# A two-block hybrid layer on one core: gated-convolution units and their projection move in between the steps of the state-space scan, dt is computed with the tokens streaming, and x is kept in DRAM meanwhile

## The reference, cut to what matters

```python
def hybrid_mixer(h, w_in, ssd_conv_w, ssd_conv_b, dt_bias, a_log, d_skip, ssd_norm_w,
                 w_ssd_proj, sconv_w, w_sconv_proj, w_o):
    u = h @ w_in
    z, xbc, dt_raw, s_b, s_c, s_x, g_a, g_b = jnp.split(u, IN_SPLITS, axis=-1)
    xbc = jax.nn.silu(causal_depthwise_conv(xbc, ssd_conv_w) + ssd_conv_b)
    xs, bm, cm = jnp.split(xbc, (SSD_INNER, SSD_INNER + SSD_GROUPS * SSD_STATE), axis=-1)
    ...
    dt = jax.nn.softplus(dt_raw.astype(jnp.float32) + dt_bias.astype(jnp.float32))
    ...
    y = ssd_chunked_scan(xs32, dt, a, bm32, cm32)
    y = y + d_skip.astype(jnp.float32).reshape(SSD_GROUPS, SSD_HPG)[..., None] * xs32
    y = y.reshape(bsz, seqlen, SSD_INNER) * jax.nn.silu(z.astype(jnp.float32))
    ...
    yg = yg * lax.rsqrt(jnp.mean(yg * yg, axis=-1, keepdims=True) + EPS)
    y = (yg.reshape(bsz, seqlen, SSD_INNER) * ssd_norm_w.astype(jnp.float32)).astype(h.dtype)
    branch_a = y @ w_ssd_proj
    v = causal_depthwise_conv(s_c * s_x, sconv_w)
    branch_b = (s_b * v) @ w_sconv_proj
    merged = jax.nn.sigmoid(g_a) * branch_a + jax.nn.sigmoid(g_b) * branch_b
    return merged @ w_o
```

## Time and profile before

| | us |
|---|---|
| median of 3 runs | 1913.37 |
| lowest and highest | 1910.51, 1920.85 |
| span of the profiled execution (first to last instruction) | 1916.4 |
| mean granted TensorE clock, share of full speed | 0.96 |
| busy in the span: TensorE, VectorE, ScalarE, GpSimd | 1783.9, 713.0, 709.4, 718.3 |

### The profile page before, as it was taken

The page is one execution under the profiler, slowest core; times in us unless marked ns, Lnnn a source line. Parts: engine busy times, 40 slices in busy tenths (PEclk is TensorE's granted clock), DMA queues, the critical chain, the costliest instruction groups (busy, mean ns, idle before and its releaser), DMA issues.

```text
span 1916.4 us, 22407 instructions
## 1 busy us (share of the span) xinstructions
PE 1783.9 (93%) x7678; PEld 1393.4 (73%) x7678; DVE 713.0 (37%) x1021; ACT 709.4 (37%) x894; POOL 718.3 (37%) x302
## 2 busy tenths in 40 slices
PE   3999797999999979999997998989899999999997
PEld 1777574888888848888875776767687788888885
DVE  5556415111110043320046988878411422222101
ACT  3455325434433342233233333433522344434322
POOL 1322033444446634444222222222444344444563
PEclk7999798999999989999898999999999999999998
DMA  8343221322223313222112111111222222222331
GB/s 324 143 154 132 99 66 44 99 89 97 88 73 97 93 66 99 88 96 94 62 55 66 59 52 56 55 44 55 77 89 99 88 88 88 90 96 82 84 97 66
DMA packets 50503, 171.93 MB, mean 90 GB/s; under 512 B 5610, under 2 KB 5866, under 8 KB 50322
## 3 DMA queue, kind: packets, MB, share of 16 engines
q1 hardware_dynamic: 50450, 171.27, 27.1%
HBM read 169.15 MB, written 2.10 MB: 89 GB/s over the span
## 4 chain that ended last, share of the span: by engine, by line
PE 80%; DVE 12%; ACT 3%; issue 3%; DMA 1%; DVEq 1%; SPq 0%; POOL 0%; ACTq 0%
PE PR L401 24%; PE PR L403 24%; PE PR L402 24%; DVE seg L1415 2%; DVE cx L1286 1%; DVE macc L1097 1%; PE AX L488 1%; DMA cond<-wcond 1%; PE AX L410 1%; PE AX L580 1%; PE AX L459 1%; PE AX L632 1%; DVE cx L1282 1%; DVE yb L1336 1%; DVE seg L1396 1%
## 5 line engine op out<-in xcount | busy, mean ns | idle before, releaser
L340 POOL TENSOR_TENSOR wlo<-raw,whi 128x1024 fp32r<-128x1024 f32 x288 | 701.8, 2438 | 1132.6 <-ACT whi L745 1132.6
L745 ACT ACTIVATE whi<-raw 128x1024 fp32r<-128x1024 f32 x288 | 302.9, 1052 | 196.3 <-PE PR L403 181.8
L401 PE MATMUL PR<-h3h,whi 128*128 128x512 f32 x640 | 263.9, 412 | 11.0 <-ACT xr L952 6.6
L402 PE MATMUL PR<-h3l,whi 128*128 128x512 f32 x640 | 256.7, 401 | 0.0
L403 PE MATMUL PR<-h3h,wlo 128*128 128x512 f32 x640 | 256.5, 401 | 0.0
L401 PEld LDWEIGHTS PR<-h3h,whi 128*128 128x128 f32 x640 | 122.6, 192 | 52.5 <-issue 20.4
L401 PE MATMUL PR<-hf1h,whi 128*128 128x512 f32 x352 | 141.1, 401 | 4.6 <-DVE hf1l L1083 3.9
L403 PEld LDWEIGHTS PR<-h3h,wlo 128*128 128x128 f32 x640 | 122.6, 192 | 29.9
L402 PEld LDWEIGHTS PR<-h3l,whi 128*128 128x128 f32 x640 | 122.8, 192 | 27.8 <-issue 0.7
L402 PE MATMUL PR<-hf1l,whi 128*128 128x512 f32 x352 | 140.6, 399 | 0.0
L403 PE MATMUL PR<-hf1h,wlo 128*128 128x512 f32 x352 | 140.4, 399 | 0.0
(11 more groups left out here) (257 smaller groups left out, 2872.0 us busy)
## 6 DMA issues: line engine op xcount, KB each, us to landing
raw<-w SPq DMA_DIRECT2D x224, 512.0 KB, 3.3
cond<-wcond SPq DMA_DIRECT2D x48, 512.0 KB, 4.3
raw<-w SPq DMA_DIRECT2D x32, 384.0 KB, 3.1
raw<-w SPq DMA_DIRECT2D x32, 320.0 KB, 2.9
x<-xin SPq DMA_DIRECT2D x1, 2048.0 KB, 7.6
out<-mixf SPq DMA_DIRECT2D x8, 256.0 KB, 2.0
con<-cons SPq DMA_DIRECT2D x1, 288.0 KB
att<-atts SPq DMA_DIRECT2D x1, 256.0 KB
```

Source lines behind the costliest of these rows:

```text
L340: pool.tensor_tensor(wlo[:, j, :], raw[:, j, :], whi[:, j, :], ALU.subtract).then_inc(lo_ready, 1)
L401: pe.matmul(bank, whi[:, j, w], oh[:, k0 + k, :], start=first and k == 0, stop=False)
L402: pe.matmul(bank, whi[:, j, w], ol[:, k0 + k, :], start=False, stop=False)
L745: act.activation(whi[:, j, :], raw[:, j, :], ACT.Copy).then_inc(hi_ready, 1)
```

## The change

- The order of the 104 mixer units is a list. First the dt sums, then B and C of group 0 and the convolution tiles 0 and 1 (8 units); then the 16 steps, each with one item of `BESIDE` between its parts: a convolution tile (3 units) in six steps, B and C of the next group in three (steps 3, 7, 11), a gate and projection unit pair in seven; then the last pair and the merge, with two g_a units in front of the first y unit.
- A step is: xs unit, `ssd_second` of the step before, first filling unit, (group start), second filling unit if there are three, z unit, `ssd_first`, last filling unit, `ssd_states`. Nothing stands at a unit's middle any more. The loops of the mixer are written out.
- dt: the weight (128x128 with zeros beside its 32 columns) is stationary and 512 tokens stream, 24 matmuls; ScalarE copies 32 rows out, four transposes turn them.
- B and C are read where they lie (bcm), without copies bt, ct, dag; bcm also takes the merge's tiles and lies where x was. So x is written to DRAM on SyncE's queue before the unit loads from 105 on and read back to x_re after the last g_a unit.
- The sum of a group's squares and `rms` move behind the next group's first step's states and behind gz.
- The output projection's first unit waits tile by tile for ml.

The diff, cut:

```diff
+BESIDE = {0: ("sc", 2), 1: ("sc", 3), 2: ("sc", 4), 3: ("bc", 1), 4: ("sc", 5), 5: ("sc", 6), 6: ("sc", 7), 7: ("bc", 2),
+          8: ("pj", 0), 9: ("pj", 1), 10: ("pj", 2), 11: ("bc", 3), 12: ("pj", 3), 13: ("pj", 4), 14: ("pj", 5), 15: ("pj", 6)}
+PARTS_OF = {"sc": ("c", "x", "b"), "bc": ("B", "C"), "pj": ("gb", "pj")}
...
 @block.sync
-            stream(U_SC, U_DN2, 32)
+            for n, (kind, m) in enumerate(MIXER):
+                first, step = W8_OF[kind]
+                load_unit(U_SC + n, (U_SC + n) % RING, w8_at(first + step * m))
+                if n == 4:
+
+                    for ready, count in (shared(res_ready, res_pool, 1, KT - 1), shared(res_ready, res_pool, 1, BY_POOL[-1])):
+                        sp.wait_ge(ready, count)
+                    sp.dma_start(x_keep[:, :, :], x[:, :, :]).then_inc(s_keep, 16)
+            for u in range(U_WO, U_WO + RING):
+                load_unit(u, u % RING, w8_at(u - 32))
+
+            sp.wait_ge(unit_used, AT["ga", KT - 1] + 1)
+            sp.wait_ge(s_keep, 16)
+            sp.dma_start(x_re[:, :, :], x_keep[:, :, :]).then_inc(s_back, 16)
+            stream(U_WO + RING, U_DN2, 32)
...
 @block.tensor
+            def dt_sums():
+
+                pe.wait_ge(dt_v, 1)
                 for k in range(KT):
+                    pe.wait_ge(*lo_part(2, k))
                     for n, (hx, wx) in enumerate(((h3h, wdth), (h3l, wdth), (h3h, wdtl))):
-                        mm = pe.matmul(AX[:, 0, 32 * c:32 * c + 32], hx[:, k, c * P:(c + 1) * P], wx[:, k, :],
-                                       start=k == 0 and n == 0, stop=k == KT - 1 and n == 2)
+                        mm = pe.matmul(AX[:, 1, :], wx[:, k, :], hx[:, k, :], start=k == 0 and n == 0,
+                                       stop=k == KT - 1 and n == 2)
+                mm.then_inc(dt_done, 1)
...
+            dt_sums()
+            mixed(("B", 0))
+            dt_turn()
+            mixed(("C", 0))
+            for name in beside("sc", 0):
+                fill(name)
+            dt_running()
+            for name in beside("sc", 1):
+                fill(name)
             pe.wait_ge(sel_ready, 1)
...
+            for s in range(STEPS):
+                extra = beside(*BESIDE[s])
+                mixed(("xs", s))
+                if s >= 1:
+                    ssd_second(s - 1)
+                fill(extra[0])
+                if s % 4 == 0:
+                    group_start(s // 4)
+                if len(extra) == 3:
+                    fill(extra[1])
+                mixed(("z", s))
+                ssd_first(s)
+                fill(extra[-1])
+                ssd_states(s)
+                if s % 4 == 0 and s >= 4:
+                    group_sum(s // 4 - 1)
+            mixed(("gb", 7))
+            ssd_second(STEPS - 1)
+            mixed(("pj", 7), vh, vl)
+            group_sum(GROUPS - 1)
+            for m in range(2):
+                mixed(("ga", m))
+            for q in range(2):
+                for m in range(2):
+                    mixed((f"A{q}", m), yh, yl, KT * q, each=lambda k: (yl_ready, KT * q + k + 1))
...
-            pe.wait_ge(ml_ready, KT)
+            pe.wait_ge(ta_ready, KT)
...
 @block.scalar
+            act.wait_ge(s_keep, 16)
+            act.wait_ge(ht_ready, 3 * KT)
+            part(("B", 0))
...
+                part(extra[0])
+                if s >= 1:
+                    v_square(s - 1)
+                if s % 4 == 0:
+                    group_start(s // 4)
+                if len(extra) == 3:
+                    part(extra[1])
+                ahead(("z", s))
+                act.activation(gz[:, :], bank(("z", s)), ACT.Tanh, scale=0.5).then_inc(thz_ready, 1)
+                if s % 4 == 1 and s >= 5:
+                    rms(s // 4 + 5, ss_ready, s // 4 + 2, width=4 * 512, bank=1)
```

More of the change, by code:

```diff
@@ L576, in _, with mixed @@
-            pe.wait_ge(dt_v, 1)
-            for c in range(NCH):
+            def mixed(name, oh=None, ol=None, k0=0, each=None):
+                kind, m = name
+                if kind != "A1":
+                    n = SUMS.index(name)
+                    if n >= 4:
+                        pe.wait_ge(*freed(SUMS[n - 4]))
+                u = AT[name]
+                unit(u, u % RING, h3h if oh is None else oh, h3l if ol is None else ol, k0, KT, bank(name),
+                     first=kind != "A1", last=kind != "A0", each=each)
@@ L584, in _ @@
-            wait = banks([(xr_ready, R0)] * 4)
-            with pe.Fori(0, 2) as i:
-                for j in range(4):
-                    wait(i, j)
-                    if j == 1:
-                        pe.wait_ge(mrg_ready, R0 + KT)
-                    unit(4 * i + (U_BC + j), j, h3h, h3l, 0, KT, PR[:, j, :])
-            pe.wait_ge(dt_v, 6)
-            for n, m in enumerate(("upto", "after", "ones")):
-                mm = pe.matmul(AX[:, 1, n * P:(n + 1) * P], con_(m), da[:, :, :].rearrange("p c h -> p (c h)"),
-                               start=True, stop=True)
@@ L727, in _ @@
                     wait(i, j)
-                    unit(4 * i + (U_WO + j), j, mh, ml, 0, KT, PR[:, j, :])
+                    unit(4 * i + (U_WO + j), j, mh, ml, 0, KT, PR[:, j, :],
+                         each=(lambda k: (ml_ready, k + 1)) if j == 0 else None)
             sum_once(V_WO + KT)
@@ L930, in _, with ahead @@
[L930 to L936 removed]
+            def ahead(name):
+                hi(0, 4, AT[name] + LEAD)
+                act.wait_ge(unit_used, AT[name] + 1)
@@ L1025, in x_square @@
+            merged(0)
+            merged(1)
+            for m in range(2, KT):
+                act.wait_ge(ta_ready, m - 1)
+                gate_a(m)
+                merged(m)
             def x_square(i, per, c, v0):
```

751 lines of the change are left out of this document (378 added, 373 removed).

## The result

| | before | after |
|---|---|---|
| median | 1913.03 us (4 runs) | 1848.76 us (4 runs) |
| lowest to highest | 1910.51 to 1920.85 | 1847.39 to 1849.11 |
| ratio, 95% interval | | 0.9649 (0.9617 to 0.968) |
| profiled execution: time, span | span 1916.4 | 1849.11, span 1846.9 |
| mixer in the profiled execution | 775.2 us | 705.3 us |

The account below looks back on a forecast made before the run. TensorE was taken to bound the kernel nearly everywhere, VectorE to pace the state-space steps. Work of 695.0 us plus 17 of waits gave a 712 us mixer, 63 below 775.2; carried to the median, 1850, range 1829 to 1882.

Parts of the forecast that it names:

- Units: Whole mixer: still 104 weight-tile units of 5.60 us each on TensorE, 582.4 us.
- Start and dt: Mixer's head: 4.3 us waiting for h3's tiles, 5.6 for 24 dt matmuls, 1.3 for transposes and running sums.
- Small matmuls of a step: State-space steps: TensorE's work besides units, 5.4 us a step, 86.4 over 16 steps; ends 5.0 and 6.17.
- Group starts: Scan: extra TensorE busy time around each group's start, 3.8 us, four times, 15 in all.
- Waits: Mixer: TensorE's new and remaining waits, found by walking each engine's order, 17 us in all.
- The spill: x stored to DRAM and loaded back: costs nothing, with 13 us of cover before TensorE needs the fourth unit.
- The wdth memsets: Ahead of ScalarE's conversions in the first down projection: free, about 3.5 us against three units.
- The rule against the change: VectorE with two SBUF inputs stands while GpSimd converts; every step now meets four to five conversions instead of two.
- Rival B: State-space steps: GpSimd hold-ups of VectorE enter every step, 2 us in each of 16, 1882; chance 0.19.
- C: Scan: ScalarE converts weights late, two tiles per step at 3.5 us, 112 over 16 steps, 1962; chance 0.05.
- D: Mixer: old waits stay in new places; only dt, running sums and merge gain, 25 us or less, 1890; chance 0.05.
- A: Mixer: the 17 us of waits shrink to a few and small matmuls cost 5.0, 1830; chance 0.15.

Follow-up runs that it names:

- the halves: Changed kernel with GpSimd's conversion of each weight unit split into two instructions of half the columns: 1842.1 us.
- the four edits: Changed kernel with norm before z unit's end, C's convolution behind scores, last squares sum before last projection product, output projection's start not awaiting last ta: 1829.4 us.
- the norm early: Changed kernel with ScalarE making the group's norm before the z unit's end, not behind z's tanh, in steps 5, 9 and 13: 1835.8 us.
- copies_filled: Changed kernel, filling kept, with VectorE's copies of B, da and C at group starts and TensorE's waits for them put back: 1857.3 us.

## Why the prediction was right, point by point

The forecast mixer was 712; the real one is 705.3. The forecast time, 1850, is only 1.2 us off, and this is luck: the forecast took 63 us from a mixer of 775.2 in a profile that lies above the median, and carried them to the median. From profile to profile the gain was 69.9, 6.7 more than forecast; from median to median 64.3.

- **Units.** 104 at 5.60: held. In the merge 96 matmuls go by in 22.40.
- **Start and dt.** Forecast 4.3 + 5.6; the stage took 9.92. Transposes and running sums took 0.95 for 1.3. The clock there is 0.73, with the first matmuls at the lower level; for most of the eight tiles the arrival of h3 sets the pace.
- **Small matmuls of a step: mis-sized.** 5.4 a step was taken; they cost 4.94, at the low end. "6.17, of which 0.62 is the visible wait" was the error: the row shows a wait of 0.62, but from the starts there L632 took 2.72 us where the same 16 matmuls take 1.51. The wait was 1.2, half of it hidden in the modelled ends. The forecast is 7 us too high here over the 16 steps. So the steps came out just below the stated 33 to 36 and 28 to 31: 32.94 and 27.34.
- **Group starts.** 15 was taken. A step with one is 36.45 against 32.94, with 0.5 of a wait: 3.0 each, 2.3 for the first: 11.4.
- **Waits.** Forecast against measured: the norm 7 and 7.0; the last sum of squares 1.7 and 1.8; the output projection 1 and 1.2; B and C steps 6 and 2.1; convolution steps 1 and 0; running sums 0.4 and none shown. The walk through the queues gave the right waits at the right lines.
- **What the waits cost beside themselves: left out.** Slow units behind the norm's waits, 5.7 us. The forecast is too high by some 16 us in small matmuls, group starts, waits and transposes, and too low by these 5.7 and by 3.8 that the terms above, 701.5 in all, leave unexplained. So the mixer's number, too, owes some of its closeness to errors of opposite sign.
- **The spill** was free as forecast, but its cover is 5.6 us and not 13: the bound is the later conversion with the least slack, and I had looked at the first only. The wdth memsets, forecast with no row beside them, take 0.91 us each, two of them.
- **The rule against the change.** The hold-ups by GpSimd did enter the steps: yb went from 1552 to 2410 ns and the states' product from 292 to 696 on average. By the Trainium skill ("SBUF — State Buffer", "SBUF: two separate sides") that is the exclusive lock, and the rows of yb and the halves agree. Rival B's time did not come, because the hold-ups fell on operations with slack and left the scores' product.
- **Rivals.** C (weights late): TensorE waited for no weight in the mixer. D (the overlap is not real): 69.9 us against its 25. A (cleaner): half of it came, small matmuls of 4.94 for its 5.0, but the norm's waits stayed; it is the kernel with the four edits that reaches its 1830.

**Where the reasoning went too far** is the diagnosis, not the sum. "VectorE, not TensorE, sets the pace" was read from one step with 16.43 us busy in 17.37. With the filling taken away, such a step is again 17.5 us with VectorE at 16.4, so for it the reading is nearly right. But TensorE and VectorE wait for each other there, in most other steps VectorE waits 1.9 to 3.2 us, and part of its load is hold-ups by GpSimd. The whole filling is worth 27 us, not the 49 to 69 that went with this reading. Undone one at a time from the changed kernel, with the mixer's length:

| undone | mixer, us | median, us |
|---|---|---|
| dt with tokens streaming | +15.1 | +15.1 |
| running sums behind a convolution tile | +12.1 | +9.8 |
| filling of the steps | +14.2 (+27.4 with the norm early) | +14.3 (+27.2) |
| B, C and da read in place | +10.0 (+18.2 without filling) | +8.5 (+18.1) |

The filling, the largest part by code, is a fifth of the gain (14.2 of 69.9), or a third with the norm early (27.4 of 83.2). The rows for dt and the running sums bring as much, but they are prices in the new order. In the old one the two stages took 18.2 and 7.5 us, where the work now takes 5.6 and 1.0: that is some 19 us of the 69.9.

The four rows add up to 51.4, not 69.9, mainly because filling and reading in place cover the same waits: taken away one after the other, with the norm early, they cost 27.4 and 18.2. The ends of the scan and of the merge were not undone. Before, they took 5.9 and 3.6 us beyond their units (17.12 and 14.84 for two units each), now 3.0 and 1.4 (19.79 for three, 124.60 for 22 units): some 5 us, by the stages and not by an experiment.

## What to carry to other kernels

A high busy share in one step is no proof that an engine sets the pace of the stage: look in every kind of step at whether it waits too, and take the other work away to see the price. Read a wait from the distance of the starts against the same group without a wait, and look at the unit behind it: 2.3 us of standing cost 4.2 in front of the running sums here. When work is moved to cover a wait, walk every engine's queue for what it now stands behind: one line of ScalarE's program in the wrong place cost 13 of the 77 us that the change could have brought.

## What the hardware showed that I had not expected

- After 2.3 us without work (and 0.5 of small transposes in front), TensorE's clock fell from 2.4 to 1.2 GHz for some 3 us: a unit took 7.25 instead of 5.70, in each of the three places (one took 8.31). After waits of 0.4 to 1.8 us in the same kernel no such unit is seen. The length of the wait alone does not decide it: of three waits of 2.4 us in the same place (copies_filled) one was followed by a slow unit, of 7.23, and two by units of 5.67.
- At the head of the mixer, behind a wait of 3.7 us, the 96 matmuls of 32 columns ran at the lower clock from first to last, 0.213 us apart, and the units behind them lost another 1.9 us. In the old order they began at 0.11 us apart behind full units, and the clock fell 2.4 us into them although TensorE never stood.
- GpSimd's conversion in two instructions takes 1.34 and 1.37 us, 0.26 more than in one, and VectorE then meets it twice: 2.41 became 1.38 and 0.69 became 1.51.
